# Gather and scatter of a block of experts' slots, each in two transfers of 64 slots instead of one of 128

## The chip, the cores and the metric

The kernel runs on one core of one Trainium2 chip. The metric is the time of one execution in device microseconds (us); lower is better. The core has a matrix engine (PE), a vector engine (DVE), an activation engine (ACT), POOL (GpSimd) and SP, a queue that here only issues transfers. Sixteen DMA engines move data between the chip's memory and the core's SBUF.

## The reference, cut to what matters

One layer of a streaming encoder for 1024 prompt frames and 64 sample frames of width 1024. After two mixers, each frame goes to two of 32 experts:

```python
h2 = rms_norm(x, norm_ffn_gain)
experts, weights = top-1 of 4 groups, then top-2 of its 8 experts
x  = x + sum over the two experts e of  weight_e * (silu(h2 @ w_gate[e]) * (h2 @ w_up[e])) @ w_down[e]
y  = rms_norm(x, norm_final_gain)
```

The weights of an expert are two matrices of 1024 x 512 and one of 512 x 1024, in float32: 6.29 MB. There are 2 x 1088 = 2176 pairs of frame and expert.

## The kernel before, in words

The change lies in `experts` (L1726 to L2147), the last large stage. Before it, the stage `merge` has written the normed rows to `h_mid`, the rows so far to `x_mid`, and a table `slot_table` with one entry for each slot: number of the frame and its weight. An expert has a block of 128 slots, filled from the front; the other slots hold a number out of bounds (NOWHERE), and an indirect transfer leaves them out. Experts with more than 128 frames would get later blocks; with this data there are none, and the stage has 32 blocks (two gathers at the start and 30 after them).

**One block.** POOL gathers 128 rows of 4 KB from `h_mid` into `x_nat` (L2088). PE turns them (L1831, in `turn_rows`), ACT and DVE split the turned rows into a high and a low part (L1938, L2023), and PE multiplies with gate and up (`gate_up`, L1843 to L1845: three products each, because of the split), then with down (`down`, L1861 to L1863) after `turn_hidden` (L1870). ACT scales the result by the slots' weights and writes it to `y_out` (`move_y`, L1954). POOL adds the rows of `y_out` to `x_mid` by an indirect scatter with addition (L2114).

**The weights.** They come in six pieces of 1 MB a block (G0, U0, G1, U1, D0, D1), issued by SP in `load_piece` (L1784), into two sets of buffers, `we_raw` for even blocks and `we_raw_odd` for odd ones. A piece is issued once PE is through with the same piece two blocks before (semaphores `gu_used`, `d_used`). ACT makes a piece's high part (L1914), DVE the low part (L2018). These, the splits above and `hidden` (L2029) are in a fixed order on each engine (`block_act`, `block_dve`): the high part of G1 of block i+1 stands before the gate of block i.

**POOL's order.** In the loop (L2133 to L2137) POOL does for each i: scatter of block i-2, gather of block i+2, then the lists of indices for the next ones: `set_scatter` (L2107) waits for the landed scatter, `set_gather` (L2094) for the landed gather. A gather waits until PE has turned the rows before it, since there is one `x_nat`; `move_y` waits for the landed scatter, since there is one `y_out`. All gathers of the loop count on the semaphore `gathered`, 16 each, all scatters on `y_scattered`.

**The lists.** At the start SP loads the table (one row for an expert). PE turns it in two transposes (L1879), ACT copies the frames' numbers as integers into `frame` (128 slots x blocks, L1982) and the weights into `share` (L1983). PE then fills its time with unused transposes (`keep_awake`, L111) until the first rows are turned. A second table for later blocks goes the same way (L1888, L1989, L1990).

**The end.** After the last but two scatters have landed (L1820, L2144), SP loads all rows of `x_mid` for the final norm, and POOL gathers the rows of the last two blocks' slots (`m_b`, `x_nat`, L2289, 128 slots each; the change leaves them alone). DVE's `add_prev` (L2251) waits for the first of these.

```python
def gather_rows(pool, at, rows, done=gathered):
    pool.indirect_dma_start(rows, None, io["h_mid"], bass.IndirectOffsetOnAxis(ap=at, axis=0),
                            bounds_check=last_frame, oob_is_err=False).then_inc(done, 16)
...
with pool.Fori(2, end - 3) as i:
    scatter_y(pool, i - 2)
    gather(pool, i + 2)
    set_scatter(pool, i - 1)
    set_gather(pool, i + 3)
```

## Time and profile before

| | us |
|---|---|
| median of 3 runs (lowest, highest) | 1682.91 (1681.29, 1684.02) |
| profiled execution, its own time | 1686.34 |
| its span, from first to last instruction | 1684.6 |
| busy: PE / DVE / ACT / POOL | 1607.2 / 1045.5 / 763.2 / 462.3 |
| expert stage, from the load of its table to the end | 1056.8 to 1684.6 |
| weight pieces (1024 KB each), median time from issue to landing | 20.0 (even), 20.5 (odd) |

A span is split by engine into busy and idle time, and an idle time has a releaser: the instruction or transfer that ended it. The chain of waits follows these back from the last instruction. PE's busy time includes its filler transposes. The DMA share is the mean busy share of the sixteen DMA engines; a queue's share is the time that its packets took, against sixteen engines' time. SP's transfers are in queue q1, POOL's in q0. Starts are us from the first instruction.

### The profile page before, as it was taken

What the parts mean: (1) busy time and instruction counts of PE and PEld (TensorE: products, weight loads), DVE (VectorE), ACT (ScalarE), POOL (GpSimd) and SP (SyncE); (2) the same over time, 40 slices, a digit from 0 to 9 for tenths busy, and PEclk for the clock granted to TensorE, in tenths of its full rate; (3) what the DMA queues carried; (4) which work ended last, traced back from release to release, by engine and by line L of the source; (5) the groups of instructions that cost most, each with busy time, mean ns of one, the idle gap of its engine ahead of it and who ended that gap; (6) DMA issues with size and microseconds to landing.
All of it is one profiled execution on the core that took longest, in us unless ns stands there. A gap on an engine that the chain in (4) does not pass through costs nothing.

```text
span 1684.6 us, 23312 instructions
## 1 busy us (share of the span) xinstructions
PE 1607.2 (95%) x8417; PEld 1316.6 (78%) x8417; DVE 1045.5 (62%) x1259; ACT 763.2 (45%) x812; POOL 462.3 (27%) x452
## 2 busy tenths in 40 slices
PE   7999999999999999998999998899999999999993
PEld 6888777777878777887888887688888887777772
DVE  5311355555655425445555555788888888888885
ACT  4310342332333322213321213488788777777773
POOL 2310354352553404321001012322222222222224
PEclk9999999999999999999999999999999999999997
DMA  7222332332230413326533346599999999999976
GB/s 256 97 92 71 125 116 73 112 92 78 66 119 32 131 42 128 132 94 240 184 122 123 130 159 272 180 356 384 371 379 378 370 377 372 369 364 372 376 255 237
DMA packets 111573, 346.45 MB, mean 206 GB/s; under 512 B 16076, under 2 KB 44924, under 8 KB 85776
## 3 DMA queue, kind: packets, MB, share of 16 engines
q1 hardware_dynamic: 101072, 327.08, 52.4%
q0 software_dynamic: 10432, 18.45, 4.3%
q8 instruction: 44, 0.72, 0.2%
q14 instruction: 25, 0.20, 0.0%
HBM read 301.90 MB, written 65.34 MB: 218 GB/s over the span
## 4 chain that ended last, share of the span: by engine, by line
PE 34%; DMA 12%; DVE 3%; issue 2%; ACT 2%; SPq 0%; POOL 0%; POOLq 0%; ACTq 0%; DVEq 0%
DMA we_raw_odd<-in_w_experts 9%; PE banks_ffn L1843 5%; PE banks_ffn L1845 5%; PE banks_ffn L1844 5%; PE banks_ffn L1324 2%; PE banks_ffn L1326 2%; PE banks_ffn L1325 2%; PE banks_ffn L1311 2%; PE banks_ffn L1313 2%; PE banks_ffn L1312 2%; PE banks_ffn L1861 2%; PE banks_ffn L1863 2%; PE banks_ffn L1862 2%; DMA we_raw<-in_w_experts 1%; PE banks_ffn L1318 1%
## 5 line engine op out<-in xcount | busy, mean ns | idle before, releaser
L994 PE MATMUL p_bank<-w_hi,ht_hi 128*128 128x512 f32 x640 | 272.9, 426 | 3.7 <-POOL w_lo L922 2.1
L996 PE MATMUL p_bank<-w_hi,ht_lo 128*128 128x512 f32 x640 | 252.9, 395 | 0.0
L995 PE MATMUL p_bank<-w_lo,ht_hi 128*128 128x512 f32 x640 | 252.3, 394 | 0.0
L2018 DVE TENSOR_TENSOR we_lo_odd<-we_raw_odd,we_hi 128x2048 fp32r<-128x2048 f32 x96 | 216.0, 2288 | 13.2 <-ACT we_hi L1914 11.8
L2018 DVE TENSOR_TENSOR we_lo<-we_raw,we_hi 128x2048 fp32r<-128x2048 f32 x96 | 215.6, 2288 | 11.8 <-ACT we_hi L1914 10.1
L1843 PE MATMUL banks_ffn<-we_hi,x_hi 128*128 128x512 f32 x512 | 206.1, 403 | 9.5 <-DVE x_lo L2023 9.5
L1914 ACT ACTIVATE we_hi<-we_raw_odd 128x2048 fp32r<-128x2048 f32 x94 | 179.0, 1918 | 58.8 <-DMA we_raw_odd<-in_w_experts 40.8
L1845 PE MATMUL banks_ffn<-we_hi,x_lo 128*128 128x512 f32 x512 | 201.0, 392 | 0.0
L1914 ACT ACTIVATE we_hi<-we_raw 128x2048 fp32r<-128x2048 f32 x90 | 171.3, 1918 | 51.6 <-DMA we_raw<-in_w_experts 38.9
L954 POOL TENSOR_TENSOR beta<-beta,prod 128x512 f32<-128x512 f32 (+3 forms) x120 | 129.5, 1091 | 223.9 <-DVE prod L806 223.9
L806 DVE TENSOR_TENSOR_SCAN prod<-keep,prod 128x512 f32<-128x512 f32 (+3 forms) x120 | 126.8, 1085 | 86.5 <-ACT keep L643 77.9
L744 DVE COPY stage<-p_bank 128x512 f32<-128x512 f32 x80 | 55.0, 687 | 155.7 <-PE p_bank L996 155.5
L994 PEld LDWEIGHTS p_bank<-w_hi,ht_hi 128*128 128x128 f32 x640 | 122.2, 191 | 30.8 <-POOL w_lo L922 5.4
L996 PEld LDWEIGHTS p_bank<-w_hi,ht_lo 128*128 128x128 f32 x640 | 121.4, 190 | 27.2
L995 PEld LDWEIGHTS p_bank<-w_lo,ht_hi 128*128 128x128 f32 x640 | 122.4, 191 | 18.9 <-issue 1.0
L922 POOL TENSOR_TENSOR w_lo<-w_raw,w_hi 128x512 fp32r<-128x512 f32 (+1 forms) x80 | 98.9, 1262 | 96.2 <-ACT w_hi L601 96.1
L1843 PEld LDWEIGHTS banks_ffn<-we_hi,x_hi 128*128 128x128 f32 x512 | 96.6, 189 | 31.6 <-issue 11.6
L643 ACT ACTIVATE keep<-z_bank 128x1024 f32<-128x1024 f32 (+3 forms) x60 | 48.6, 810 | 152.4 <-PE z_bank L1054 83.7
L1845 PEld LDWEIGHTS banks_ffn<-we_hi,x_lo 128*128 128x128 f32 x512 | 96.5, 188 | 21.0
L2114 POOL DMA_INDIRECT x_mid<-y_out,scatter_at x30 | 76.5, 2550 | 96.8 <-ACT y_out L1954 70.6
L1861 PE MATMUL banks_ffn<-we_hi,a_hi 128*128 128x512 f32 x256 | 100.6, 393 | 0.0
L1844 PE MATMUL banks_ffn<-we_lo_odd,x_hi 128*128 128x512 f32 x256 | 100.5, 392 | 0.0
(355 smaller groups left out, 3022.6 us busy)
## 6 DMA issues: line engine op xcount, KB each, us to landing
we_raw<-in_w_experts SPq DMA_DIRECT2D x96, 1024.0 KB, 20.0
we_raw_odd<-in_w_experts SPq DMA_DIRECT2D x96, 1024.0 KB, 20.5
w_raw<-in_w_main SPq DMA_DIRECT2D x80, 256.0 KB, 4.6
projected<-stage SPq DMA_DIRECT2D x80, 256.0 KB, 2.0
gates<-projected SPq DMA_DIRECT2D x9, 1024.0 KB, 4.9
qkvr<-projected SPq DMA_DIRECT2D x9, 768.0 KB, 4.2
o_nat<-mixed SPq DMA_DIRECT2D x9, 512.0 KB, 3.3
x_mid<-x_new SPq DMA_DIRECT2D x9, 512.0 KB, 2.9
```

The lines of the kernel that those rows point to most:

```text
L806: dve.tensor_tensor_scan(prod[:, h, at:at + n * P][:, ::-1], line, line, prod[:, h, at + n * P:at + n * P + 1], ALU.mult, ALU.min).then_in ...
L922: pool.tensor_tensor(w_lo[:, n % SLICES, cols], w_raw[:, n % SLICES, cols], w_hi[:, n % SLICES, cols].bitcast(F32), ALU.subtract).then_inc ...
L954: pool.tensor_tensor(beta[:, u % 2, h, 0:n * P], beta[:, u % 2, h, 0:n * P], prod[:, h, at + 1:at + 1 + n * P], ALU.mult).then_inc(weighed, 1)
L994: pe.matmul(out, ht_hi[:, k, rows], w_hi[:, j], start=(k == 0), stop=False)
L995: pe.matmul(out, ht_hi[:, k, rows], w_lo[:, j], start=False, stop=False)
L996: last = pe.matmul(out, ht_lo[:, k, rows], w_hi[:, j], start=False, stop=(k == KD - 1))
L1843: pe.matmul(out, x_hi[:, k], w_hi[:, j, cols], start=(k == 0), stop=False)
L1844: pe.matmul(out, x_hi[:, k], w_lo[odd][:, j, cols], start=False, stop=False)
L1845: last = pe.matmul(out, x_lo[:, k], w_hi[:, j, cols], start=False, stop=(k == KD - 1))
L1861: pe.matmul(out, a_hi[:, k], w_hi[:, j, cols], start=(k == 0), stop=False)
L1914: act.activation(w_hi[:, j], w_raw[odd][:, j], ACT.Copy).then_inc(high[j], 1)
L2018: dve.tensor_tensor(w_lo[odd][:, j], w_raw[odd][:, j], w_hi[:, slot].bitcast(F32), ALU.subtract).then_inc(split[slot], 1)
```

## The change

Each gather and each adding scatter of a block is issued as two transfers of 64 slots. The indices of both halves must stand on partitions 0 to 63, so a second list `half_frame` (64 x 2 x blocks) is made beside `frame`, which the final stage still reads; two more transposes and one more copy for each of the two tables make it. Where ACT made `frame` first, it now makes `half_frame` first, which releases POOL, and then `frame`. The semaphores of gathers and scatters count 32 a block.

```diff
+    half_frame = sb("half_frame", [P // 2, 2, BLOCKS + 1], I32)
+    gather_at, scatter_at = sb("gather_at", [P // 2, 2], I32), sb("scatter_at", [P // 2, 2], I32)
...
+    halves = banks[0:P // 2, 7, P:P + 2 * EXPERTS].rearrange("p (a e) -> p a e", a=2)
+    halves_later = banks[0:P // 2, 7, 2 * P:2 * P + 2 * LATER].rearrange("p (a e) -> p a e", a=2)
...
-            pe.wait_ge(gathered, i * 16)
+            pe.wait_ge(gathered, i * 32)
...
         pe.wait_ge(table_in, 16)
         for a in range(2):
+            slots = slice(a * (P // 2), (a + 1) * (P // 2))
+            pe.transpose(halves[:, a], table[:, slots, 0], s.ident[0:EXPERTS, 0:EXPERTS]).then_inc(table_turned, 1)
+        for a in range(2):
             pe.transpose(listed[:, a], table[:, :, a], s.ident[0:EXPERTS, 0:EXPERTS]).then_inc(table_turned, 1)
...
         for a in range(2):
+            slots = slice(a * (P // 2), (a + 1) * (P // 2))
+            pe.transpose(halves_later[:, a], later[:, slots, 0], s.ident[0:LATER, 0:LATER]).then_inc(later_turned, 1)
             pe.transpose(listed_later[:, a], later[:, :, a], s.ident[0:LATER, 0:LATER]).then_inc(later_turned, 1)
...
-        act.wait_ge(table_turned, 2)
-        act.activation(frame[:, 0:EXPERTS], listed[:, 0], ACT.Copy).then_inc(frame_ready, 1)
+        act.wait_ge(table_turned, 4)
+        act.activation(half_frame[:, :, 0:EXPERTS], halves, ACT.Copy).then_inc(frame_ready, 1)
+        act.activation(frame[:, 0:EXPERTS], listed[:, 0], ACT.Copy).then_inc(share_ready, 1)
...
-        act.activation(frame[:, EXPERTS:], listed_later[:, 0], ACT.Copy).then_inc(later_frame, 1)
+        act.activation(half_frame[:, :, EXPERTS:], halves_later, ACT.Copy).then_inc(later_frame, 1)
+        act.activation(frame[:, EXPERTS:], listed_later[:, 0], ACT.Copy).then_inc(later_share, 1)
...
         def gather_rows(pool, at, rows, done=gathered):
-            pool.indirect_dma_start(rows, None, io["h_mid"], bass.IndirectOffsetOnAxis(ap=at, axis=0),
-                                    bounds_check=last_frame, oob_is_err=False).then_inc(done, 16)
+            for a in range(2):
+                half = slice(a * (P // 2), (a + 1) * (P // 2))
+                pool.indirect_dma_start(rows[half], None, io["h_mid"], bass.IndirectOffsetOnAxis(ap=at[:, a], axis=0),
+                                        bounds_check=last_frame, oob_is_err=False).then_inc(done, 16)
...
-            pool.tensor_copy(gather_at[:], frame[:, bass.ds(i, 1)]).then_inc(gather_set, 1)
+            pool.tensor_copy(gather_at[:].unsqueeze(2), half_frame[:, :, bass.ds(i, 1)]).then_inc(gather_set, 1)
...
-            pool.indirect_dma_start(io["x_mid"], bass.IndirectOffsetOnAxis(ap=scatter_at[:], axis=0), y_out, None,
-                                    bounds_check=last_frame, oob_is_err=False, compute_op=ALU.add).then_inc(y_scattered, 16)
+            for a in range(2):
+                half = slice(a * (P // 2), (a + 1) * (P // 2))
+                pool.indirect_dma_start(io["x_mid"], bass.IndirectOffsetOnAxis(ap=scatter_at[:, a:a + 1], axis=0),
+                                        y_out[half], None, bounds_check=last_frame, oob_is_err=False,
+                                        compute_op=ALU.add).then_inc(y_scattered, 16)
...
-        gather_rows(pool, frame[:, 0:1], x_nat, first_gathered)
-        gather_rows(pool, frame[:, 1:2], x_second)
+        gather_rows(pool, half_frame[:, :, 0:1], x_nat, first_gathered)
+        gather_rows(pool, half_frame[:, :, 1:2], x_second)
```

The left-out lines change counts of semaphores (16 to 32 a block, two to four transposes, one to two copies) and the scatter's list in the same way as the gather's.

## Rows read from the trace of the kernel before

**Rows 1.** Chain of waits, from 1040 us on: start, length, what.
```profile
1315.28 0.44 PE banks_ffn L1870 x4
...
1333.00 0.44 PE banks_ffn L1870 x4
...
1342.73 20.12 DMA we_raw_odd<-in_w_experts
...
1378.61 21.41 DMA we_raw_odd<-in_w_experts
...
1565.32 21.52 DMA we_raw_odd<-in_w_experts
```

**Rows 2.** Stretches: length, busy us (instructions) per engine, PE clock, DMA busy share, GB/s.
```profile
1200.00:1250.00 50.00, 50.00 (x236) 41.51 (x235) 44.33 (x26) 40.45 (x29) 12.90 (x12) 1.00 1.00 377
...
1616.00:1622.00 6.00, 6.00 (x32) 5.08 (x31) 5.29 (x4) 5.44 (x6) 2.56 (x1) 1.00 0.51 204
...
1641.20:1642.20 1.00, 0.52 (x3) 0.10 (x3) 0.84 (x5) 1.00 (x2) 0.00 (x0) 1.00 0.48 94
```

**Rows 3.** PE's timeline, 1609 to 1660 us: start, length, instruction.
```profile
1629.27 0.66 PE L1870 MATMUL banks_ffn<-ident,hidden 128*128 128x128 f32 x4
...
1647.80 0.60 PE L1870 MATMUL banks_ffn<-ident,hidden 128*128 128x128 f32 x4
```

**Rows 4.** DMA view, 1100 to 1200 us: packets; issues with median us to landing.
```profile
DMA packets 6168, 37.03 MB, mean 370 GB/s; under 512 B 1325, under 2 KB 1325, under 8 KB 1975
...
we_raw<-in_w_experts SPq DMA_DIRECT2D x18, 1024.0 KB, 9.8
```

**Rows 5.** DMA view, 1440 to 1540 us; queue: packets, MB, share of 16 engines.
```profile
DMA packets 6220, 37.14 MB, mean 371 GB/s; under 512 B 1260, under 2 KB 1260, under 8 KB 2114
...
q0 software_dynamic: 1597, 3.50, 14.2%
...
we_raw<-in_w_experts SPq DMA_DIRECT2D x14, 1024.0 KB, 23.6
```

**Rows 6.** DMA view, 1466 to 1470 us, with weights alone.
```profile
DMA packets 224, 1.65 MB, mean 412 GB/s; under 512 B 23, under 2 KB 23, under 8 KB 23
```

**Rows 7.** The gathers' line: ns min/median/max, first and last start.
```profile
L2088 POOL DMA_INDIRECT x_nat<-h_mid,gather_at x30: 1029/1334/3066, 1079.0 to 1602.6; - x30
```

**Rows 8.** Timeline of POOL, then of PE, over one undisturbed block.
```profile
1301.36 2.55 POOL L2114 DMA_INDIRECT x_mid<-y_out,scatter_at  x1 [3.30 <-ACT y_out L1954]
1305.21 2.54 POOL L2088 DMA_INDIRECT x_nat<-h_mid,gather_at  x1 [1.30 <-PE banks_ffn L1831]
1312.75 0.18 POOL L2107 COPY scatter_at<-frame 128x1 int32 x1 [5.00 <-DMA x_mid<-y_out,scatter_at]
1316.49 0.18 POOL L2094 COPY gather_at<-frame 128x1 int32 x1 [3.56 <-DMA x_nat<-h_mid,gather_at]
...
1321.05 1.03 PE L1831 MATMUL banks_ffn<-ident,x_nat 128*128 128x128 f32 x8
```

**Rows 9.** POOL's timeline: second scatter of slot numbers, 64 rows.
```profile
1053.85 1.87 POOL L1640 DMA_INDIRECT slot_table<-entry,slot  x1 [0.31 <-issue]
```

**Rows 10.** Timeline around the start of the expert stage.
```profile
1058.63 0.39 PE L1879 MATMUL banks_ffn<-ident,table 32*128 32x32 f32 x2 [3.82 <-DMA table<-slot_table]
...
1058.95 5.16 PE L111 MATMUL banks_ffn<-ident 128*128 128x128 f32 x30
...
1059.53 1.05 POOL L2088 DMA_INDIRECT x_nat<-h_mid,frame  x1 [3.81 <-ACT frame L1982]
...
1063.95 1.04 PE L1831 MATMUL banks_ffn<-ident,x_nat 128*128 128x128 f32 x8
```

**Rows 11.** Chain of waits in the tail.
```profile
1635.97 6.98 DMA x_mid<-y_out,scatter_at
...
1643.83 9.40 DMA m_b<-x_mid,slot_at
...
1653.25 1.23 DVE m_b L2251
```

More of the change, by code:

```diff
@@ L1751, in experts @@
     frame, share = sb("frame", [P, BLOCKS + 1], I32), sb("share", [P, BLOCKS + 1])
-    gather_at, scatter_at = sb("gather_at", [P, 1], I32), sb("scatter_at", [P, 1], I32)
+    half_frame = sb("half_frame", [P // 2, 2, BLOCKS + 1], I32)
+    gather_at, scatter_at = sb("gather_at", [P // 2, 2], I32), sb("scatter_at", [P // 2, 2], I32)
     gu = banks[:, 0:2]
@@ L1819, in sync @@
         sp.sem_inc(rows_begun, 1)
-        sp.wait_ge(y_scattered, end * 16 - 32)
+        sp.wait_ge(y_scattered, end * 32 - 64)
         sp.sem_inc(rows_begun, 1)
@@ L1825, in turn_rows @@
         if first:
-            pe.wait_ge(first_gathered, 16)
+            pe.wait_ge(first_gathered, 32)
         else:
-            pe.wait_ge(gathered, i * 16)
+            pe.wait_ge(gathered, i * 32)
             pe.wait_ge(x_low, i)
@@ L1952, in move_y @@
         if not first:
-            act.wait_ge(y_scattered, i * 16)
+            act.wait_ge(y_scattered, i * 32)
         act.activation(y_out, y[:], ACT.Copy, scale=share[:, bass.ds(i, 1)]).then_inc(done or y_moved, 1)
@@ L1987, in scalar @@
         block_act(act, 1, 1, y_before=False, first_down=True)
-        act.wait_ge(later_turned, 2)
-        act.activation(frame[:, EXPERTS:], listed_later[:, 0], ACT.Copy).then_inc(later_frame, 1)
+        act.wait_ge(later_turned, 4)
+        act.activation(half_frame[:, :, EXPERTS:], halves_later, ACT.Copy).then_inc(later_frame, 1)
+        act.activation(frame[:, EXPERTS:], listed_later[:, 0], ACT.Copy).then_inc(later_share, 1)
         act.activation(share[:, EXPERTS:], listed_later[:, 1], ACT.Copy).then_inc(later_share, 1)
-        act.wait_ge(share_ready, 1)
-        act.wait_ge(later_share, 1)
+        act.wait_ge(share_ready, 2)
+        act.wait_ge(later_share, 2)
         block_act(act, 2, 0, first_y=True)
@@ L2087, in gather_rows @@
         def gather_rows(pool, at, rows, done=gathered):
-            pool.indirect_dma_start(rows, None, io["h_mid"], bass.IndirectOffsetOnAxis(ap=at, axis=0),
-                                    bounds_check=last_frame, oob_is_err=False).then_inc(done, 16)
+            for a in range(2):
+                half = slice(a * (P // 2), (a + 1) * (P // 2))
+                pool.indirect_dma_start(rows[half], None, io["h_mid"], bass.IndirectOffsetOnAxis(ap=at[:, a], axis=0),
+                                        bounds_check=last_frame, oob_is_err=False).then_inc(done, 16)
         def set_gather(pool, i):
-            pool.wait_ge(gathered, i * 16 - 16)
-            pool.tensor_copy(gather_at[:], frame[:, bass.ds(i, 1)]).then_inc(gather_set, 1)
+            pool.wait_ge(gathered, i * 32 - 32)
+            pool.tensor_copy(gather_at[:].unsqueeze(2), half_frame[:, :, bass.ds(i, 1)]).then_inc(gather_set, 1)
         def gather(pool, i):
@@ L2100, in gather @@
             pool.sem_inc(gather_begun, 1)
-            gather_rows(pool, gather_at[:], x_nat)
+            gather_rows(pool, gather_at[:].unsqueeze(2), x_nat)
         def set_scatter(pool, i, first=False):
             if not first:
-                pool.wait_ge(y_scattered, i * 16)
-            pool.tensor_copy(scatter_at[:], frame[:, bass.ds(i, 1)]).then_inc(scatter_set, 1)
+                pool.wait_ge(y_scattered, i * 32)
+            pool.tensor_copy(scatter_at[:].unsqueeze(2), half_frame[:, :, bass.ds(i, 1)]).then_inc(scatter_set, 1)
         def scatter_y(pool, i):
@@ L2143, in gpsimd @@
         scatter_y(pool, end - 3)
-        pool.wait_ge(y_scattered, end * 16 - 32)
+        pool.wait_ge(y_scattered, end * 32 - 64)
         pool.sem_inc(slots_begun, 1)
```

## The prediction

> **What bounds the kernel now.** I read the chain of waits first, then the PE's own timeline, the stretches, the DMA view in short windows, POOL's timeline, and last the tail. The change lies wholly in the expert stage, from 1059 us on.
>
> In the chain the turn of the hidden rows (L1870), once a block, stands at 1315.28 and 1333.00: 17.72 us a block, with the PE busy throughout [rows 1, 2]. Until 1342.73 the chain is PE alone. From there a weight transfer of 20 to 22 us stands in it once in two blocks; from 1378.61 to 1565.32 it returns five times, 37.34 us a pair or 18.67 us a block [rows 1]. So the first half of the stage is PE-bound and the second is bound by the weights' arrival. L1870 of block 14 stands at 1333.00 and that of block 31 at 1647.80 [rows 1, 3]: 314.80 us for 17 blocks, where 17 x 17.72 is 301.24. **13.56 us are lost to late weights**; at block 30 (1629.27) it is 12.75.
>
> Why late: a piece took 9.8 us to land at 1100 to 1200 and 23.6 us at 1440 to 1540 [rows 4, 5]. The DMA falls behind the PE by about 1 us a block from the start, and the PE feels it once landing passes 20 us. The DMA's mean rate is about 377 GB/s, its mean busy share 1.00 [rows 2].
>
> Is that the whole of the hardware's rate? Three rows say no. Where weights move alone, the rate is 412 GB/s [rows 6]. In 1616 to 1622, with no weights left on some engines while others still owe theirs, the share is 0.51 [rows 2]. In 1641.2 to 1642.2 the last scatter is alone, and the share is 0.48: close to eight of sixteen engines [rows 2]. A block holds 50 to 80 real frames in 128 slots, the rest being out of bounds: 650 packets of 4 KB in 100/17.72 = 5.6 blocks is 58 frames a block (each frame is one packet in and one out), and 854 in 5.4 blocks is 79 [rows 4, 5]. Nearly all lie in slots 0 to 63. I read this as: the first 64 slots go to one half of the engines, eight slots each, and the other half gets only what lies behind slot 64. The landing of a 1 MB weight piece waits for the busiest engine.
>
> The Trainium skill (DMA: Bandwidth & Descriptors, "The descriptor swizzle") gives just such a map for 128 partitions: engines 0 to 7 write partitions 0 to 63. The trace agrees (0.48 and 0.51).
>
> **The sum for the busiest engine.** Weights: 6.29 MB a block at 412 GB/s, 15.3 us. The rest of 18.67 is 3.4 us for eight rows in and eight rows out. The sixteen engines' mean for these rows is 14.2% of 18.67 = 2.7 us in the fullest stretch [rows 5], so 5.3 on one half would be its upper bound.
>
> **What the change does.** (1) Each gather and scatter of a block becomes two of 64 slots. If 64 slots are spread over sixteen engines, four each, an engine carries four rows of the first half and up to four of the second: 15.3 + 1.7 = 17.0 us where a block has 64 frames or fewer, up to 18.67 on the few engines that get the second half's first rows, where a block has 68 or more. Blocks of 58 frames run the DMA 0.7 us ahead of the PE, blocks of 79 let it fall 0.95 us behind. Over the stage these nearly cancel; in the full stretch from 1440 on, nine blocks could add 8.5 us to a landing that starts at about 9.8: 18 us, still under 20. So I take **all 13.56 us of PE waiting as gone**. The rows show no heavy transfer of 64 slots; bounds are 0 (halves keep the old engines) and 13.56. I choose the upper end, since at an even spread only the fullest blocks stay above 17.72.
>
> The Trainium skill (same page, "Why a DMA increments its semaphore by 16 and not by 1") says that a transfer uses the largest number of engines up to 16 that divides its slowest dimension: 16 for 64 slots. No row here shows it.
>
> (2) POOL issues. A scatter's issue takes 2.55 us and a gather's 1.33 (1.03 to 3.07) [rows 7, 8]; plain scatters of 64 slots took 1.87 us beside DVE's weight work [rows 9], so I cannot count on half. Two issues cost from the same in sum (plus 0.31 between them) to double: +0.6 to +5.7 us a block. Behind them on POOL stand the two copies of lists, which wait for landings anyway. Cover: the gather's landing is seen at 1316.49, and PE turns the rows at 1321.05: 4.56 us [rows 8]. POOL's own time is no limit: its next scatter comes 18 us after this one, and four issues in full are 11 us. And the first half moves while the second is issued, with half as many rows for an engine. I take 2 us more in issuing, nothing on the path.
>
> (3) Start. Two more transposes precede the first list: two of 32 rows take 0.39 us [rows 10], so +0.3 with the copy to the integer list. The first gather lands after two issues: 1.05 + 0.31 more, less about half the moving time. It had been issued at 1059.53, and the PE turned at 1063.95 right behind its filler work, which slides with the transposes [rows 10]. Between +0.3 and +1.6; I take +0.6. The two extra transposes of the later lists, in the PE's stream, +0.2. The extra ACT copies (0.2 us each) lie beside PE work. Copies of 64 x 2 instead of 128 x 1 indices: nothing, hidden in POOL's waits; uncovered, some 0.1 us. The semaphore counts double and wait for the same events.
>
> (4) Tail. In an undisturbed block POOL issues the scatter at 1301.36, 3.80 us behind L1870 (1315.28 - 17.72); at block 30 it came 6.70 behind (1635.97 against 1629.27), since ACT stood waiting for a late weight piece [rows 1, 3, 8, 11]. With L1870 at 1616.52 the last waited scatter is issued at 1620.32 instead of 1635.97. It landed in 6.98 us on an emptying queue [rows 11] and in 11.39 between weights (1301.36 to 1312.75) [rows 8]; I take 9.2, as the queue is fuller now but rows per engine fewer. Then 0.88 of waiting and the gather of the last slots, 9.40, untouched by the change [rows 11]: add_prev at 1639.8, against 1653.25, is 13.4 us earlier. The PE's last turn is 13.56 earlier. The gather binds: -13.4, bounds -15.6 to -11.2.
>
> Sum: -13.4 + 0.6 + 0.2 = **-12.6 us**. The profiled execution (1686.34 us, span 1684.6) goes to 1673.7; it lies 3.4 above the median of the runs, 1682.91, which goes to **1670.3**.
>
> **Rivals.**
> - Partial (1677). The second halves keep the same first engines at eight rows in full blocks; if landing is higher at 1440 than I think, the PE stalls again from there and half of the loss (6.5 us) stays. For: 79 frames a block in that stretch. Against: the lighter stretches before it.
> - Nothing (1683.7). The halves stay on the engines of their partitions, or the rate is not set by the busiest engine; then only the start costs, +0.8. For: the busy share of 1.00 throughout looks like no engine idles. Against: 0.48 and 0.51 in the tail.
> - By the Trainium skill (same page, "Where 436 GB/s comes from"), the memory side binds HBM loads near 358 GB/s, whatever the spread: this rival again. The trace speaks against it: 412 GB/s.
> - Slower (1701). POOL's doubled issues. If the second ones cost in full (2.55 + 2.54 + 2 x 0.31 = 5.71 us) and the gather's landing moves with them, the rows come 1.15 us behind L1831's need in each of 28 blocks: +32, less the 13.6 of waits that this replaces. It decides from 4.56 us of extra delay on. For: issues beside DVE's work take up to 3 us. Against: the transfer itself shortens.
> - That the change doesn't split anything can't be: the issues are separate instructions.
>
> **Chances.** Forecast 0.68 (its own range 1666 to 1674.5), partial 0.12, nothing 0.11, slower 0.09. The range to 1680.5 takes in the first two. A difference of 0.2% (3.4 us) is about what a measurement of this kernel can tell from none: faster 0.80, same 0.11, slower 0.09.
>
> **What would show it.** In the changed profile: L1870 every 17.72 us to the end; weight pieces landing in under 20 us throughout; no weight transfer in the chain before the tail; the share in the tail well over 0.5 until the queue is empty; a gather landing before L1831 needs it. It is wrong if landing still climbs 1 us a block (the spread did not change), or if PE waits before L1831 (POOL).

## The result, and the profile after

The changed kernel takes **1688.11 us** (median of 20 runs, 1684.1 to 1693.8) against 1684.24 for the kernel before (20 runs, 1681.15 to 1688.77) on the same chip: a ratio of 1.0027, 95% interval [1.0018, 1.0035]. The forecast was 1670.3 with a range to 1680.5 and 0.09 on slower. It was wrong in sign as well as in size.

| profiled execution | before | after |
|---|---|---|
| span | 1684.6 | 1685.7 |
| POOL busy | 462.3 | 571.5 |
| weight pieces, median landing, whole page (even / odd) | 20.0 / 20.5 | 15.0 / 15.4 |
| 1200 to 1400 us: landing of even pieces, mean rate | 19.4, 375 GB/s | 14.3, 377 GB/s |
| first to last L1870 (after: L1873) | 566.3 | 566.8 |

The last row is the one to follow through this text. The turn of the hidden rows happens once a block, 32 times, so from its first start to its last start lie 31 blocks (and 0.8 us within the last four transposes). The view of that line, with min/median/max in ns and the first and the last start, of the kernel before:

```profile
L1870 PE MATMUL banks_ffn<-ident,hidden x128: 270/272/331, 1081.8 to 1648.1; 128*128 128x128 f32 x128
  DVE hidden L2029: 9.7, 16
```

and of the kernel after (the second line is how long, and how often, PE stood idle ahead of it until DVE had made `hidden`):

```profile
L1873 PE MATMUL banks_ffn<-ident,hidden x128: 270/272/329, 1080.0 to 1646.8; 128*128 128x128 f32 x128
  DVE hidden L2039: 18.3, 18
```

The stage's length did not shrink: 566.3 before, 566.8 after, where the forecast had 13.56 less. That is 0.5 of the 3.9 us between the medians. The start costs 0.7 more (step 3 below), and in these two profiles the part from the last hidden turn to the end is 2.4 us longer (1648.1 to 1684.6, then 1646.8 to 1685.7). No run isolates that part; it differs as much between other kernels below (36.6 us in e9, 39.2 in e5). What holds the stage shows in the chain of waits of the kernel after, which answers to [rows 1, 11]: start, length, what.

```profile
1399.68 22.90 DMA we_raw_odd<-in_w_experts
...
1453.69 26.60 DMA we_raw<-in_w_experts
...
1511.49 26.72 DMA we_raw_odd<-in_w_experts
...
1563.89 21.91 DMA we_raw_odd<-in_w_experts
...
1607.02 23.05 DMA we_raw<-in_w_experts
...
1637.10 4.00 DMA x_mid<-y_out,scatter_at
...
1643.34 9.48 DMA x_final<-x_mid
```

Late weights are still the bound of the second half. They come into the chain at 1399.68 instead of at 1342.73, and then with longer transfers (up to 26.72 us instead of 21.52). The DMA views of 1100 to 1200 and 1440 to 1540 us, as [rows 4, 5]:

```profile
we_raw<-in_w_experts SPq DMA_DIRECT2D x17, 1024.0 KB, 8.9
```

```profile
we_raw<-in_w_experts SPq DMA_DIRECT2D x15, 1024.0 KB, 24.8
```

A piece lands a little sooner at first (8.9 against 9.8) and not at all sooner in the full stretch (24.8 against 23.6). The stretches, with the columns of [rows 2]:

```profile
1200.00:1250.00 50.00, 50.00 (x240) 41.62 (x239) 44.34 (x27) 41.07 (x30) 21.54 (x17) 1.00 1.02 376
...
1616.00:1622.00 6.00, 6.00 (x32) 5.01 (x31) 5.75 (x4) 5.58 (x5) 3.64 (x2) 1.00 0.66 242
...
1622.00:1626.00 4.00, 4.00 (x19) 3.33 (x18) 4.00 (x3) 3.44 (x3) 0.68 (x1) 1.00 0.48 135
```

The share in the emptying queue is 0.66 and then 0.48, where an even spread should have kept it near 1 until nothing is left. By the packet records, 8 to 9 weight packets were in flight from 1617 to 1621 us, against 7 in the kernel before. So about half of the engines were still behind the other half, although the rows were now spread. That is the first hint that the split's rows slow some engines' weights.

POOL was not the reason. Its timeline over one block, as [rows 8], then PE's:

```profile
1298.91 2.38 POOL L2129 DMA_INDIRECT x_mid<-y_out,scatter_at  x1 [2.72 <-ACT y_out L1962]
1301.60 1.90 POOL L2129 DMA_INDIRECT x_mid<-y_out,scatter_at  x1 [0.30 <-issue]
1303.80 1.45 POOL L2101 DMA_INDIRECT x_nat<-h_mid,gather_at  x1 [0.30 <-issue]
1305.56 1.89 POOL L2101 DMA_INDIRECT x_nat<-h_mid,gather_at  x1 [0.30 <-issue]
...
1313.89 0.18 POOL L2107 COPY gather_at<-half_frame 64x2 int32 x1 [3.72 <-DMA x_nat<-h_mid,gather_at]
```

```profile
1319.37 1.03 PE L1834 MATMUL banks_ffn<-ident,x_nat 128*128 128x128 f32 x8
```

The rows of the next block are seen landed at 1313.89 and PE takes them at 1319.37: 5.48 us in hand, more than the 4.56 before, with no idle time ahead of L1834 in the block.

### The profile page after: what moved, and what is told of

It is laid out like the page before. It is cut to its first block, busy times and chain, and to the rows that moved or that the text cites. A ratio compares the mean times of both kernels' runs of the same rounds, so it can differ in the third digit from the quotient of the medians.

```text
span 1685.7 us, 23384 instructions
## 1 busy us (share of the span) xinstructions
PE 1603.3 (95%) x8421; PEld 1315.6 (78%) x8421; DVE 1044.8 (62%) x1259; ACT 762.8 (45%) x814; POOL 571.5 (34%) x514
## 4 chain that ended last, share of the span: by engine, by line
PE 36%; DMA 9%; DVE 3%; issue 2%; ACT 1%; POOL 0%; SPq 0%; POOLq 0%; DVEq 0%; ACTq 0%
PE banks_ffn L1846 5%; PE banks_ffn L1848 5%; PE banks_ffn L1847 5%; DMA we_raw_odd<-in_w_experts 4%; DMA we_raw<-in_w_experts 3%; PE banks_ffn L1866 2%; PE banks_ffn L1864 2%; PE banks_ffn L1865 2%; PE banks_ffn L1324 2%; PE banks_ffn L1326 2%; PE banks_ffn L1325 2%; PE banks_ffn L1311 2%; PE banks_ffn L1313 2%; PE banks_ffn L1312 2%; PE banks_ffn L1318 1%
## 5 line engine op out<-in xcount | busy, mean ns | idle before, releaser
L2028 DVE TENSOR_TENSOR we_lo<-we_raw,we_hi 128x2048 fp32r<-128x2048 f32 x96 | 215.5, 2287 | 10.4 <-ACT we_hi L1922 9.2
L2129 POOL DMA_INDIRECT x_mid<-y_out,scatter_at x60 | 128.4, 2140 | 95.1 <-ACT y_out L1962 85.9
L2101 POOL DMA_INDIRECT x_nat<-h_mid,gather_at x60 | 101.4, 1689 | 24.5 <-issue 17.7
## 6 DMA issues: line engine op xcount, KB each, us to landing
we_raw_odd<-in_w_experts SPq DMA_DIRECT2D x96, 1024.0 KB, 15.4
```

The lines of the kernel that those rows point to most:

```text
L2028: dve.tensor_tensor(w_lo[odd][:, j], w_raw[odd][:, j], w_hi[:, slot].bitcast(F32), ALU.subtract).then_inc(split[slot], 1)
L2101: pool.indirect_dma_start(rows[half], None, io["h_mid"], bass.IndirectOffsetOnAxis(ap=at[:, a], axis=0), bounds_check=last_frame, oob_is_e ...
L2129: pool.indirect_dma_start(io["x_mid"], bass.IndirectOffsetOnAxis(ap=scatter_at[:, a:a + 1], axis=0), y_out[half], None, bounds_check=last_ ...
```

## The experiments

The theories, with the letters that the expectations use. **A**: the busiest DMA engine sets the weights' arrival, and spreading rows is worth the 13 us. **B**: the limit is shared by all engines, so spreading is worth nothing. **C**: with the split it is the size of the first transfer (up to 64 rows on all engines at once) or a slower group of engines that costs. **D/E**: what costs is the place: in a transfer of 64 neighbouring slots an engine writes rows into partitions whose weights another engine writes (E), or all of a transfer goes into one half of the partitions (D). **F**: two gathers at work on all engines cost wherever they write. (In the expectations of e5 and e7, F is narrower, the issue and completion of more transfers, and E takes even and odd slots, too, for partitions of other engines.)

All results in one place. "Length" is first to last start of the hidden turn, "landing" the median of even weight pieces in 1200 to 1400 us; the ratio is to the kernel before on the same chip. Length and landing are read from one profiled execution of each kernel.

| kernel | gather | scatter | frames of an expert in | median us | ratio, 95% interval | length | landing |
|---|---|---|---|---|---|---|---|
| before | whole | whole | first slots | 1684.24 | 1 | 566.3 | 19.4 |
| after | halves | halves | first slots | 1688.11 | 1.0027 [1.0018, 1.0035] | 566.8 | 14.3 |
| e1 | whole | whole | 0, 64, 1, 65 ... | 1668.91 | 0.9892 [0.9866, 0.9917] | 551.9 | 7.8 |
| e2 | no rows | no rows | | 1667.35 | 0.9888 [0.9859, 0.9918] | 551.9 | 4.8 |
| e3 | halves | whole | first slots | 1707.80 | 1.0132 [1.0108, 1.0155] | 587.0 | 23.6 |
| e4 | whole | halves | first slots | 1668.57 | 0.9901 [0.9878, 0.9924] | 552.0 | 8.8 |
| e5 | even/odd | whole | first slots | 1686.57 | 1.0011 [1.0001, 1.0021] | 566.3 | 19.3 |
| e7 | quarters | whole | first slots | 1708.82 | 1.0147 [1.0132, 1.0162] | 593.2 | 15.2 (odd) |
| e8 | even/odd | whole | by eights | 1689.94 | 1.0039 [1.0022, 1.0056] | 566.8 | 19.2 |
| e9 | halves | whole | by fours | 1692.67 | 1.0048 [1.0031, 1.0066] | 573.4 | 20.7 |
| e10 | even/odd | even/odd | by eights | 1692.23 | 1.0055 [1.0035, 1.0076] | 566.3 | 18.9 |
| e11 | even/odd | whole | by fours | 1669.38 | 0.9897 [0.9878, 0.9916] | 551.9 | 7.5 |
| e12 | even/odd | even/odd | by fours | 1671.41 | 0.9907 [0.9887, 0.9928] | 551.9 | 7.6 |
| e13 | halves | halves | by fours | 1729.48 | 1.0267 [1.0242, 1.0292] | 602.9 | 25.0 |
| e14 | halves | whole | by pairs | 1682.14 | 0.9987 [0.9973, 1.0001] | 562.3 | 13.6 |
| e15 | halves | halves | by pairs | 1686.39 | 1.0014 [1.0000, 1.0027] | 563.2 | 12.6 |

### Is it the busiest engine? (e1, e2)

e1 keeps the whole transfers of the kernel before and only changes where an expert's frames stand: its frames go in turn to the slots 0, 64, 1, 65 and so on.

```diff
+        act.wait_ge(table_in, 16)
+        act.activation(evened.rearrange("e (h q) a -> e h q a", h=2),
+                       table[:].rearrange("e (q h) a -> e h q a", h=2), ACT.Copy).then_inc(even_made, 1)
...
-            pe.transpose(listed[:, a], table[:, :, a], s.ident[0:EXPERTS, 0:EXPERTS]).then_inc(table_turned, 1)
+            pe.transpose(listed[:, a], evened[:, :, a], s.ident[0:EXPERTS, 0:EXPERTS]).then_inc(table_turned, 1)
```

> Before's kernel with whole transfers of 128 slots, but with an expert's frames dealt in turn to slots 0, 64, 1, 65 and so on, so that the rows of a block lie evenly on both halves of the slots (one more ACT copy at the start, some 0.5 us). Theory A (the busiest DMA engine sets the landing of weights, and the split gave its gain back through its extra transfers): L1870 every 17.72 us to the end, 10 to 13 us faster than before. Theory B (a limit shared by all sixteen engines sets it, so that the spread of the rows doesn't matter): within 3 us of before, weight pieces again landing in 22 us and more by the end. Theory C (the busiest engine sets it, but rows cost the same wherever they are, and eight of the engines are slower anyway): a gain of 3 to 6 us.

e2 takes the rows away: from block 2 on the gathers' lists, and all scatters' lists, hold only numbers out of bounds, so the experts' results are not added to the output.

```diff
-            pool.tensor_copy(gather_at[:], frame[:, bass.ds(i, 1)]).then_inc(gather_set, 1)
+            pool.tensor_copy(gather_at[:], gone[:, bass.ds(i, 1)]).then_inc(gather_set, 1)
```

> Before's kernel in which the gathers and added scatters of blocks 2 and on are still issued, but all their indices are out of bounds, so that no row moves (left out: the experts' sum for nearly all frames). All theories: the weights alone take less than 17.72 us a block, so PE is never held by them, 12 to 14 us faster than before. It shows whether eight of the sixteen DMA engines still finish late without any rows: Theory A says no (share near 1 until the weights queue is empty), Theory C says yes (share near 0.5 for some us).

The view of the hidden turn's line in e1:

```profile
L1872 PE MATMUL banks_ffn<-ident,hidden x128: 270/272/331, 1083.0 to 1634.9; 128*128 128x128 f32 x128
  DVE hidden L2034: 5.0, 2
```

and in e2:

```profile
L1871 PE MATMUL banks_ffn<-ident,hidden x128: 270/272/328, 1083.8 to 1635.7; 128*128 128x128 f32 x128
  DVE hidden L2032: 5.0, 2
```

Both have a length of 551.9 us, PE's own pace: only 2 idle times ahead of the line, against 16 before. With no rows at all the stage is no shorter than with rows spread well. So 566.3 - 551.9 = 14.4 us were to be had, the forecast's 13.56 was the right size, and **theory A holds**: spreading the same packets, with the same number of transfers, wins 1.1%. B falls. (Both medians are 16 to 18 us under the one before, a little more than the 10 to 13 and 12 to 14 expected.)

e2 also answers whether eight engines are slower by themselves. Its weights' queue empties on all engines together:

```profile
1606.00:1610.00 4.00, 4.00 (x23) 3.41 (x22) 4.00 (x3) 2.57 (x2) 1.78 (x2) 1.00 0.02 2
```

The share is 0.02 there, and by the packet records the weight packets in flight go from 16 at 1604.5 to none at 1605.5, where the kernel before keeps 7 from 1617 to 1621. So that part of C falls too: the late half is late because of the rows.

The Trainium skill (DMA: Bandwidth & Descriptors, "Where 436 GB/s comes from") has the memory side bind loads near 358 GB/s. The trace does not agree: the kernel before moved 412 GB/s with weights alone [rows 6], and e1 383 on average over 1200 to 1400 us with its gathers and scatters counted in. The measurement decides.

### Which half of the change costs? (e3, e4)

e3 is the kernel after with the scatter made whole again, e4 with the gather made whole again.

```diff
-            for a in range(2):
-                half = slice(a * (P // 2), (a + 1) * (P // 2))
-                pool.indirect_dma_start(io["x_mid"], bass.IndirectOffsetOnAxis(ap=scatter_at[:, a:a + 1], axis=0),
-                                        y_out[half], None, bounds_check=last_frame, oob_is_err=False,
-                                        compute_op=ALU.add).then_inc(y_scattered, 16)
+            pool.indirect_dma_start(io["x_mid"], bass.IndirectOffsetOnAxis(ap=scatter_at[:], axis=0), y_out, None,
+                                    bounds_check=last_frame, oob_is_err=False, compute_op=ALU.add).then_inc(y_scattered, 16)
```

> The changed kernel with the gathers in two transfers of 64 slots and the scatters back in one of 128. Theory A: half of the extra transfers gone and half of the balance kept: between before and the change, 0 to +4 us against before. Theory B: as before within 3 us. If one of the two splits alone carries the loss of 4 us, this kernel or the next shows it.

> The changed kernel with the scatters in two transfers of 64 slots and the gathers back in one of 128. Theory A: 0 to +4 us against before. Theory B: as before within 3 us; since a packet of the adding scatter takes twice as long as one of a gather, its split should matter more, in either direction, than that of the gathers.

The hidden turn's line in e3:

```profile
L1873 PE MATMUL banks_ffn<-ident,hidden x128: 270/272/332, 1082.7 to 1669.7; 128*128 128x128 f32 x128
  DVE hidden L2039: 37.5, 31
```

and in e4:

```profile
L1873 PE MATMUL banks_ffn<-ident,hidden x128: 270/272/328, 1077.9 to 1629.9; 128*128 128x128 f32 x128
  DVE hidden L2039: 5.0, 2
```

Every theory had both kernels between -3 and +4 us of the one before; they came out at +22.9 and -16.4. The two parts of the change have opposite signs. **The scatter's split alone wins the whole forecast** (552.0 us, 1668.57), even with the gather's rows still on one half of the engines. **The gather's split alone loses** (587.0, 1707.80): 20.7 us more in the stage than before. Together they nearly cancel, as the kernel after shows (566.8). The plain sum, 566.3 + 20.7 - 14.3, would be 572.7: e4 cannot show more than 14.4, since PE's own pace stops it at 551.9, while beside the split gather the split scatter is worth 587.0 - 566.8 = 20.2.

What the split gather does to the weights can be read in a window of 2 us beside a gather's rows, 1309 to 1311 us, where q1 is the weights' queue. In the kernel after:

```profile
DMA packets 105, 0.56 MB, mean 279 GB/s; under 512 B 18, under 2 KB 18, under 8 KB 56
...
q1 hardware_dynamic: 56, 0.40, 75.2%
```

q1's 0.40 MB are 49 packets of 8 KB; they took 75.2% of 16 engines' 2 us, so 0.49 us each. e1 in the same window:

```profile
q1 hardware_dynamic: 90, 0.66, 78.8%
```

0.66 MB are 81 packets, at 0.31 us each. The weights' packets themselves become slow while the rows of a split gather land.

One window can mislead, so here is the mean over the blocks from 1120 to 1330 us, of the 8 KB packets that start 4.5 to 9 us behind a gather's first issue, by the packet records. With the gather in neighbouring halves it is 0.37 to 0.42 us (e13, e9, e3, e14, e15, the kernel after, in this order), with quarters 0.36 (e7). In all others it is 0.33 to 0.34 (before, e2, e5, e8, e10) or 0.31 (e1, e4, e11, e12).

### The place, or the split itself? (e5, e7 to e15)

e5 is e3 with one expression changed in the gather and the making of its lists: a transfer has the even slots or the odd ones, so it still has 64 slots and there are still two.

```diff
-                half = slice(a * (P // 2), (a + 1) * (P // 2))
+                half = slice(a, P, 2)
                 pool.indirect_dma_start(rows[half], None, io["h_mid"], bass.IndirectOffsetOnAxis(ap=at[:, a], axis=0),
```

> The kernel with the split gathers and whole scatters, but the two halves of a gather are the even and the odd slots, so that each transfer of 64 rows is written across all 128 partitions instead of into one half of them. Theory D (each engine of an unsplit transfer writes only partitions of its own; a half written by all sixteen engines into 64 partitions meets the weights' writes there, and the weight packets slow down while it lasts): the weight packets beside a gather take 0.31 to 0.33 us as beside an unsplit one, and the time is at or under that of before, 1675 to 1687 us. Theory E (it is enough that an engine writes partitions other than its own, wherever): weight packets beside a gather still take 0.4 us and more, and the time stays 15 to 25 us over before. Theory F (the second transfer's issue and completion cost it): as E in time, with weight packets at 0.31 to 0.33 us.

e7 is e3 with four gathers of 32 neighbouring slots.

```diff
-            for a in range(2):
-                half = slice(a * (P // 2), (a + 1) * (P // 2))
+            for a in range(4):
+                half = slice(a * (P // 4), (a + 1) * (P // 4))
```

> The same kernel with each gather in four transfers of 32 slots, each written by all engines into 32 partitions. Theory D: the conflict is denser, weight packets beside a gather take longer than the 0.38 to 0.39 us of the halves, and the time is over that of the halves (1.013 of before): 1.015 to 1.04. Theory E: as the halves, 1.010 to 1.016. Theory F: four issues cost twice what two do: 1.02 to 1.03, with weight packets no slower than beside halves.

e5 lost nothing: its length, 566.3, and its landing, 19.3, are those of the kernel before. But its frames still fill the first slots, so its spread may be as poor as before, and it does not tell D/E from F. e7 answered another question. The view of the line that turns the gathered rows:

```profile
its engine sat idle before it (us, times) until:
  DMA x_nat<-h_mid,gather_at: 63.9, 40
```

PE waited 63.9 us for gathers, and its waits ahead of the hidden turn are only 5.0 us in 2 times: with four issues a block POOL is late, the way of the prediction's slower rival, and weights no longer bind. At 1400 us POOL goes from one block's gathers to the next in 20.0 us: the issues, the landing (8.3 us behind the last issue), the copy of the list and the scatter's issue follow each other. The two transfers of the real change stay below the point from which that decides; four pass it. So e7's time says nothing on the weights, and its weight packets (0.36 us) do not bear out D, which had them over the 0.38 of the halves.

To have both places with an even spread, the frames were dealt, first over groups of eight slots (e8, e10) and over groups of four in each half (e9). The deal of e8 and e10, then of e9:

```diff
+        for a in range(2):
+            act.activation(evened[:, :, a].rearrange("x (e c h) -> x e c h", e=16, h=2),
+                           table[:, :, a].rearrange("x (c e h) -> x e c h", e=16, h=2), ACT.Copy).then_inc(even_made, 1)
```

```diff
+            act.activation(evened[:, :, a].rearrange("x (h e c) -> x e c h", e=16, h=2),
+                           table[:, :, a].rearrange("x (c e h) -> x e c h", e=16, h=2), ACT.Copy).then_inc(even_made, 1)
```

> The gather in two transfers of 64 slots, the even slots and the odd ones, so that each transfer writes partitions over the whole of x_nat and a row lands in the partition group whose weights the same engine writes; the frames of an expert are dealt so that either transfer has about 34 rows, about two on each of the 16 engines; the scatter is whole. The parity gather without the dealing took 1686.6, as the kernel before. Theory D/E (what costs is that rows are written into partitions that another engine's weights own, or into one half at a time): nothing of that is here and all engines are busy alike, so it is as fast as the evenly dealt whole gather: 1669 (1665 to 1673), the 8 KB weight packets beside a gather at 0.31 to 0.33 us. Rival F (what costs is having two gathers at work on all 16 engines, wherever they write): as slow as the split gather, 1695 to 1710, weight packets of 0.37 us and over beside a gather.

> The same dealing idea and the same number of rows on each engine and in each transfer as in the parity kernel, but the two transfers are slots 0 to 63 and 64 to 127: only the partitions that an engine writes to differ. Theory D/E: slow again, 1690 to 1710, weight packets beside a gather at 0.37 us and over. Rival C (the split gather was slow because its first transfer is full, 64 rows at once, and its second nearly empty): about 1669 like the even dealing, weight packets 0.31 to 0.33 us.

> The kernel after with three edits: gather and scatter in even and odd slots instead of lower and upper ones, and frames dealt evenly over the engines in either. Theory D/E: the gather costs nothing beside the weights any more and the scatter keeps its gain: 1668 (1663 to 1672), PE's blocks at 17.7 us to the end. Rival F: 1685 or more, as the kernel after.

Taken at their word, the times of e8 (1689.94) and e10 (1692.23) spoke for F and against D/E, though their weight packets (0.33 to 0.34 us) stayed under F's 0.37. e9 (1692.67, packets of 0.38) came out as D/E had it. But e8's length, 566.8, and landing, 19.2, were once more those of the kernel before, as if nothing had been spread. Its deal fills the first four of every eight slots. If an engine has every eighth group of four slots, that leaves half of the engines idle. The Trainium skill (DMA: Bandwidth & Descriptors, "The descriptor swizzle") gives such a map for 128 partitions, with groups of four. The traces agree, by the packets of the last waited scatter (81 rows, alone on the engines): in e8 12 to 13 are in flight and then 8 to 9, as in the kernel before; in e9 and e11, which fill two slots of every four, 16. My deal by eights had ignored it.

e11 and e12 deal by fours: the first 64 frames go to the slots 0, 1, 4, 5, ... 124, 125, the next ones to 2, 3, 6, 7 and so on. e11 is otherwise e8, e12 otherwise e10; e13 has this deal with lower and upper halves.

```diff
+        act.activation(evened.rearrange("x (g c h) t -> x c g (h t)", g=32, h=2),
+                       table[:].rearrange("x (c g h) t -> x c g (h t)", g=32, h=2), ACT.Copy).then_inc(even_made, 1)
```

> The parity gather again (even slots in one transfer, odd ones in the other, scatter whole), but with the frames dealt over groups of FOUR slots: the first 64 frames go to the slots 0, 1, 4, 5, 8, 9, and so on to 125, the next ones to 2, 3, 6, 7. The dealing of the last round filled the first four of every eight slots, and if an engine owns every eighth group of four slots, that left half of the engines without rows; its weight packets beside a gather were those of the kernel before. Now every engine has about four rows by any of these maps, two in each gather. Theory D/E (the partitions that the gather writes to are what costs): 1669 (1664 to 1673), PE's blocks at 17.7 us to the end, the mean 8 KB weight packet beside a gather at 0.31 to 0.33 us. Rival F (two gathers on all 16 engines cost wherever they write): 1690 and over, weight packets of 0.37 us and over.

> The kernel after, with gather and scatter in even and odd slots and the frames dealt over groups of four slots. Theory D/E: 1667 (1662 to 1671), as fast as the even dealing. Rival F: 1685 or more, as the kernel after.

> The kernel after with that dealing alone: gather and scatter in lower and upper slots, each transfer with about 34 rows, two on each engine. It differs from the run before only in which 64 partitions each transfer has. Theory D/E: slow, 1685 to 1695, weight packets beside a gather of 0.37 us and over. Rival C (64 rows at once in the first transfer are what costs): 1669, weight packets of 0.31 to 0.33 us. Rival F: 1685 or more, as the run before.

The hidden turn's line in e11:

```profile
L1875 PE MATMUL banks_ffn<-ident,hidden x128: 270/272/328, 1083.6 to 1635.5; 128*128 128x128 f32 x128
  DVE hidden L2044: 5.0, 2
```

and in e8:

```profile
L1875 PE MATMUL banks_ffn<-ident,hidden x128: 270/272/445, 1083.7 to 1650.5; 128*128 128x128 f32 x128
  DVE hidden L2045: 12.1, 18
```

The two kernels differ in the deal alone, and 1.4% lies between them. So **F falls**: a gather in two transfers, rows on all engines, costs nothing (551.9) if each transfer has the even or the odd slots. e12, with the scatter split the same way, has the same length.

e13 was far slower than the 1685 to 1695 of D/E. The hidden turn's line in it:

```profile
L1875 PE MATMUL banks_ffn<-ident,hidden x128: 270/273/332, 1081.6 to 1684.5; 128*128 128x128 f32 x128
  DVE hidden L2044: 57.6, 38
```

In a transfer of 64 slots this deal again left engines idle. I counted the packets of 4 KB in flight, from the packet records. At the start of the stage, where gathers move nearly alone, e9 and e13 had 8 or fewer for most of the time (with peaks to 10 and 12, as these two blocks hold 77 rows each and not 64), against up to 15.7 in the kernel after, whose first half is full. In the last waited scatter, e13's second transfer kept 7 to 9 in flight. Two slots of every four filled and half of the engines at work: that fits an engine taking a transfer's slots in pairs. So e9 and e13 mix two harms, and a cleaner pair was needed. e14 (e3) and e15 (the kernel after) deal over pairs: the even slots of both halves first, then the odd ones.

```diff
+        for a in range(2):
+            act.activation(evened[:, :, a].rearrange("x (h p c) -> x c p h", p=32, c=2),
+                           table[:, :, a].rearrange("x (c p h) -> x c p h", p=32, c=2), ACT.Copy).then_inc(even_made, 1)
```

> Gather in lower and upper slots, scatter whole, with the frames dealt over the even slots of either half first, then over the odd ones: about 34 rows in each transfer, and if a transfer of 64 slots gives an engine its slots in pairs, every engine has two of them; 12 to 16 packets at work at a time where the first gathers are alone. Theory D/E (rows written to partitions whose weights another engine writes): 1690 to 1710, weight packets beside a gather at 0.37 us and over. Rival C (64 rows at once): 1669, packets of 0.31 to 0.33 us.

> The kernel after with that dealing. D/E: 1680 to 1695, like the kernel after and 10 to 25 us slower than the parity kernel with the same edit to the scatter (1671). Rival C: 1669. If engines were to take slots otherwise than in pairs: 1729 again.

In e14 the packets in flight at the start peaked at 14.0 (means over half a microsecond), as in e11 (14.4), and the second transfer of e15's last waited scatter had up to 16: the spread is now the same. The hidden turn's line in e14:

```profile
L1875 PE MATMUL banks_ffn<-ident,hidden x128: 270/272/421, 1082.8 to 1645.1; 128*128 128x128 f32 x128
  DVE hidden L2045: 12.8, 15
```

and in e15:

```profile
L1875 PE MATMUL banks_ffn<-ident,hidden x128: 270/272/332, 1081.9 to 1645.1; 128*128 128x128 f32 x128
  DVE hidden L2045: 13.8, 16
```

**This pair is the decisive one.** e14 against e11: the same number of transfers, of slots in each, of rows in each (about 34) and of engines at work. By the two deals even the same frames stand in the same order in each gather; only the partitions differ. 562.3 against 551.9 us; ratios 0.9987 [0.9973, 1.0001] against 0.9897 [0.9878, 0.9916]. With the scatter split too, e15 against e12: 563.2 against 551.9, ratios 1.0014 against 0.9907, intervals again apart. e13 against e10 is nearly such a pair too, with half of the engines idle in both: 602.9 against 566.3. e14 came out 8 us below the 1690 that was expected at least, e15 inside its 1680 to 1695. And e15 (1.0014) is close to the kernel after (1.0027), whose first transfer has up to 64 rows at once: the full first transfer, what is left of theory C, is worth a few microseconds at most (566.8 against 563.2).

A window of 1.5 us beside a gather shows it in single packets, e14 from 1278.0 to 1279.5 us:

```profile
DMA packets 109, 0.50 MB, mean 330 GB/s; under 512 B 33, under 2 KB 33, under 8 KB 64
...
q1 hardware_dynamic: 55, 0.37, 86.0%
```

and e11 from 1279.1 to 1280.6 us:

```profile
DMA packets 138, 0.63 MB, mean 418 GB/s; under 512 B 52, under 2 KB 52, under 8 KB 71
...
q1 hardware_dynamic: 78, 0.55, 87.4%
```

q1's 0.37 MB are some 45 packets of 8 KB; 86.0% of 24 us (16 engines, 1.5 us) makes 0.46 us each. In e11 0.55 MB are 67, and 87.4% of 24 us makes 0.31 us each, the time that they take undisturbed. These windows lie beside the densest rows; block by block, the means from 4.5 to 9 us behind a gather's first issue are 0.38 to 0.44 us in e14 and 0.31 to 0.32 in e11.

## Why the prediction was wrong, point by point

- **What bounds the kernel, and why: right.** Weights late on the busier half of the engines. e1 and e2 put 14.4 us on it; the forecast said 13.56. Had only the scatter been split, the forecast of 1670.3 would nearly have come out (e4, 1668.57).
- **Step (1), the failing step.** "An engine carries four rows of the first half and up to four of the second: 15.3 + 1.7 = 17.0 us". It took for granted that a row costs an engine the same time wherever it is written, and that the 15.3 us of weights stay 15.3. For the scatter, which reads SBUF, that held: e4 at 552.0, and 562.3 against 563.2 from e14 to e15, where weights do bind. For the gather, which writes it, it did not: the weights' packets beside it went from 0.31 (e11) to 0.46 us (e14) in the densest windows, and from 0.31 to 0.40 in the mean. The term that was missing is some 11 us of stage (e14 minus e11: 10.4; e15 minus e12: 11.3), and more where the weights have no slack left: e11's pieces land in 7.5 us and e14's in 13.6 before PE feels it. As for the whole change, the kernel after has 14.9 over e12. The other 3.6 us lie between it and e15, which differs in the deal alone: up to 64 rows in the first transfer and an uneven second one. So the 14.4 us to be had and the 14.9 lost leave the length as it was.
- The bounds given for this step were 0 and 13.56. A loss was left out with no reason: the rule of the Trainium skill (DMA: Bandwidth & Descriptors, "Why a DMA increments its semaphore by 16 and not by 1") on how many engines 64 slots use was read, and where those engines then write was not asked. The trace agrees with that rule: 16 packets in flight in either transfer of e15's last scatter.
- **Step (2), POOL: right.** A pair of scatter issues takes 2.38 + 0.30 + 1.90 = 4.58 us where one took 2.55 [rows 8], a pair of gathers 1.45 + 0.30 + 1.89 = 3.64 where the median was 1.33 [rows 7]: 4.3 us more. I had taken 2 us, within bounds of 0.6 to 5.7, and it was hidden all the same. The rows lie 5.48 us ahead of need.
- **Step (3), the start: right.** From the first transpose of the table to the turn of the first rows it was 5.32 us before (1058.63 to 1063.95) [rows 10] and is 6.00 now (1056.10 to 1062.10, below). That is +0.7; the forecast had +0.6.
- **Step (4), the tail: wrong in its parts.** The last waited scatter was issued from 1634.37 on (its second half at 1637.10) instead of at 1620.32, since the weights were late. It landed 6.7 us behind its first issue, where I took 9.2. I had the gather `m_b` bind; in the kernel after the load of `x_final` stands in the chain instead (1643.34, 9.48 us). The tail was to come 13.4 us earlier and gained nothing.
- **The rivals.** "Partial" and "nothing" had the right observable (late weights remain) with the wrong reason (old engines kept, or a shared limit). "Slower" by POOL did not happen with two transfers, but its mechanism is real: e7 met it with four. The slower way that did happen was not among them.

The timeline at the start of the kernel after, for step (3):

```profile
1056.10 0.30 PE L1883 MATMUL banks_ffn<-ident,table 32*64 32x32 f32 x2 [3.85 <-DMA table<-slot_table]
...
1057.16 0.99 POOL L2101 DMA_INDIRECT x_nat<-h_mid,half_frame  x1 [4.00 <-ACT half_frame L1990]
...
1062.10 1.04 PE L1834 MATMUL banks_ffn<-ident,x_nat 128*128 128x128 f32 x8
```

**What stays open.** That the place of the writes costs is shown; why is not. The Trainium skill (SBUF — State Buffer, "Door 1: The DMA port swizzle") says that a group of four partitions and the one 32 further on share one of sixteen ports, and the descriptor swizzle named above has each engine write one port alone in a 128-partition transfer. By that, if an engine takes a transfer's slots in pairs and engines 0 to 7 take its first 32, a gather of even or odd slots keeps each engine to its own port, and one of neighbouring slots sends pairs to ports that other engines' weights use. It fits e11, e14 and e4 (reads are untouched), but no trace here names an engine or a port. Nor was E told from D: no kernel wrote to other engines' partitions spread over all 128. And e3's loss of 20.7 us, twice that of e14 over e11, is not taken apart: the kernel before has no slack to lose, and e3's first gather is full.

## What to carry to other kernels

Before spreading an indirect transfer over more engines, ask two things: which engines the slots that really move will use, and which partitions each will write beside the bulk load. Here the cheapest cure was no split at all, but dealing an expert's frames to slots on both sides (e1, 1.1% faster than before); splitting only the scatter (e4) gives the same, and a split gather has to interleave its slots (e12) rather than cut them in halves. A change with two like parts should be costed, and run, one part at a time: run alone, they were worth +20.7 and -14.3 us here.

## What the runs showed of the hardware that was not expected

- An 8 KB weight packet takes 0.31 us, and 0.46 to 0.49 us where the rows of a gather into 64 neighbouring partitions land most densely (e14, and the kernel after); beside the same rows in a gather of every second partition it stays at 0.31 (e11).
- The scatter with addition shows no such effect when split into neighbouring halves (e4: 552.0 us, as with no rows at all; e15 against e14, where weights bind: 563.2 against 562.3).
- In a transfer of 128 slots an engine's share goes by groups of four slots (last scatter: 8 to 9 packets in flight in e8 behind the first rows, 16 in e9 and e11), in one of 64 slots apparently by pairs (7 to 9 in the second transfer of e13's last scatter, up to 16 in e15's).
- Idle engines and misplaced writes together cost far more than apart: 51.0 us of stage (e13 over e12), where idle engines alone cost 14.4 (e10) and misplaced writes alone 11.3 (e15). Apart, PE's own pace hides a part of each. e13 is 2.7% slower than before, the slowest of all.
